# SBUF placement of the streamed and the stationary operands in a two-stack transformer kernel

## What is computed

```python
# first_block, 2 layers
a = rms_norm(h, attn_norm[i]); proj = a @ w_in[i]
mix = concat([diff_attention(...), ssd_mixer(...), gla_mixer(...)])
h = h + mix @ w_out[i]
f = rms_norm(h, ffn_norm[i])
h = h + (silu(f @ w_ffn_gate[i]) * (f @ w_ffn_up[i])) @ w_ffn_down[i]
h = h + sigmoid(h @ ple_w_gate[i]) * (p[i] @ ple_w_proj[i])
# second_block, 4 layers (stick-breaking, MoBA, sliding window, stick-breaking)
mod = silu(c) @ ada_w[i] + ada_b[i]            # shift, scale, gate, twice
x = x + g1 * attention(modulate(rms_norm(x), sh1, sc1))
x = x + g2 * swiglu(modulate(rms_norm(x), sh2, sc2), w_gate, w_up, w_down)
```

## Time and profile before

| | |
|---|---|
| median of 3 runs | 2531.91 us (2529.34 to 2535.33) |
| the profiled execution's own time | 2530.38 us |
| its span, first to last instruction | 2528.6 us |
| mean granted TensorE clock | 0.933 of full |
| PE busy | 92% of the span |
| PEld busy | 85% |
| DVE busy | 59% |
| ACT busy | 40% |
| DMA | 56% of 16 engines, 173 GB/s |

### The profile page before, as it was taken

The page is one execution under the profiler, slowest core; times in us unless marked ns, Lnnn a source line. Parts: engine busy times, 40 slices in busy tenths (PEclk is TensorE's granted clock), DMA queues, the critical chain, the costliest instruction groups (busy, mean ns, idle before and its releaser), DMA issues.

```text
span 2528.6 us, 44727 instructions
## 1 busy us (share of the span) xinstructions
PE 2320.7 (92%) x17136; PEld 2153.3 (85%) x17136; DVE 1500.3 (59%) x2564; ACT 1020.5 (40%) x1670; POOL 0.2 (0%) x4
## 2 busy tenths in 40 slices
PE   5799899988798899899899989899978899998998
PEld 4687699987786799879899978799966799897998
DVE  4533178845431488836688876587866555566554
ACT  3412244414321344325544444444444444455443
POOL 0000000000000000000000000000000000000000
PEclk8989799998988899999899989899988899998999
DMA  4344179962433299844389954389932366443664
GB/s 130 96 108 108 34 243 297 305 198 84 125 85 101 68 306 301 276 122 129 94 268 303 300 161 125 98 289 296 289 113 68 118 191 192 124 133 100 191 193 139
DMA packets 553295, 436.26 MB, mean 173 GB/s; under 512 B 31824, under 2 KB 479352, under 8 KB 553080
## 3 DMA queue, kind: packets, MB, share of 16 engines
q1 hardware_dynamic: 549840, 431.35, 56.0%
q10 hardware_dynamic: 3368, 3.71, 0.5%
HBM read 433.96 MB, written 1.05 MB: 172 GB/s over the span
## 4 chain that ended last, share of the span: by engine, by line
PE 84%; DVE 7%; ACT 3%; DMA 2%; issue 2%; DVEq 1%; ACTq 1%; SPq 0%
PE bank L575 12%; PE bank L576 12%; PE bank L577 12%; PE acc L575 6%; PE acc L576 6%; PE acc L577 6%; PE bank L561 6%; PE bank L702 5%; PE acc L620 3%; PE bank L980 2%; PE bank L779 2%; PE bank L585 1%; PE bank L570 1%; PE bank L745 1%; PE bank L691 1%
## 5 line engine op out<-in xcount | busy, mean ns | idle before, releaser
L575 PE MATMUL bank<-h_hi,w_hi 128*128 128x256 f32 x2704 | 775.0, 287 | 27.4 <-DVE h_lo L1251 15.2
L576 PE MATMUL bank<-h_lo,w_hi 128*128 128x256 f32 x2704 | 761.6, 282 | 0.0
L577 PE MATMUL bank<-h_hi,w_lo 128*128 128x256 f32 x2704 | 760.4, 281 | 0.0
L1013 ACT ACTIVATE w_hi<-wslot 128x1024 fp32r<-128x1024 f32 x510 | 531.3, 1056 | 509.8 <-PE acc L577 261.5
L1429 DVE TENSOR_TENSOR w_lo<-wslot,w_hi 128x1024 fp32r<-128x1024 f32 x396 | 474.7, 1221 | 229.5 <-ACT w_hi L1013 229.1
L575 PEld LDWEIGHTS bank<-h_hi,w_hi 128*128 128x128 f32 x2704 | 520.6, 193 | 46.6 <-issue 31.9
L576 PEld LDWEIGHTS bank<-h_lo,w_hi 128*128 128x128 f32 x2704 | 522.4, 193 | 0.0
L577 PEld LDWEIGHTS bank<-h_hi,w_lo 128*128 128x128 f32 x2704 | 521.9, 193 | 0.0
L575 PE MATMUL acc<-mid_hi,w_hi 128*128 128x256 f32 x1056 | 299.0, 283 | 0.8 <-DVE mid_lo L1662 0.8
L576 PE MATMUL acc<-mid_lo,w_hi 128*128 128x256 f32 x1056 | 295.5, 280 | 0.0
L577 PE MATMUL acc<-mid_hi,w_lo 128*128 128x256 f32 x1056 | 295.2, 280 | 0.0
(11 more groups left out here) (255 smaller groups left out, 2688.4 us busy)
## 6 DMA issues: line engine op xcount, KB each, us to landing
wslot<-in_ada_w_dram SPq DMA_DIRECT2D x192, 512.0 KB, 5.9
wslot<-in_ffn_w_gate_dram SPq DMA_DIRECT2D x88, 512.0 KB, 4.7
wslot<-in_ffn_w_up_dram SPq DMA_DIRECT2D x88, 512.0 KB, 5.4
wslot<-in_ffn_w_down_dram SPq DMA_DIRECT2D x88, 512.0 KB, 3.6
wslot<-in_w_in_dram SPq DMA_DIRECT2D x72, 512.0 KB, 4.1
wslot<-in_sb_w_in_dram SPq DMA_DIRECT2D x48, 512.0 KB, 4.6
wslot<-in_w_ffn_gate_dram SPq DMA_DIRECT2D x44, 512.0 KB, 4.9
wslot<-in_w_ffn_up_dram SPq DMA_DIRECT2D x44, 512.0 KB, 5.5
```

The source lines that it names most:

```text
L575: pe.matmul(dst, w_hi[:, w, cols], hi, start=start, stop=False, skip_group_check=True)
L576: pe.matmul(dst, w_hi[:, w, cols], lo, start=False, stop=False, skip_group_check=True)
L577: return pe.matmul(dst, w_lo[:, w, cols], hi, start=False, stop=stop, skip_group_check=True)
L1013: return act.activation(dst, src, ACT.Copy)
```

## The change

The order of the `sb(...)` calls is changed; no instruction, shape, wait or transfer is added or removed. Sizes rounded up to 32 bytes, small tiles move between the streamed families.

```diff
-        cum = sb("cum", [P, 8])
         mid_hi = sb("mid_hi", [P, 2, S], F32R)
         mid_lo = sb("mid_lo", [P, 2, S], F32R)
-        wend = sb("wend", [P, 4])
+        dt_bias = sb("dt_bias", [P, DEPTH, 8])
+        a_neg = sb("a_neg", [P, DEPTH, 8])
+        h_lo = sb("h_lo", [P, KT, S], F32R)
+        sinks = sb("sinks", [P, 16])
+        a_log = sb("a_log", [P, DEPTH, 8])
         h_hi = sb("h_hi", [P, KT, S], F32R)
-        h_lo = sb("h_lo", [P, KT, S], F32R)
-        wexp = sb("wexp", [P, 4])
+        skip_all = sb("skip_all", [P, DEPTH, 8])
+        lam = sb("lam", [P, DEPTH, 4])
+        neg_lam = sb("neg_lam", [P, DEPTH])
         y_hi = sb("y_hi", [P, 512], F32R)
         y_lo = sb("y_lo", [P, 512], F32R)
-        epst = sb("epst", [P, 1])
+        da_gain = sb("da_gain", [P, DEPTH])
+        skip = sb("skip", [P, DEPTH, 4])
         w_hi = sb("w_hi", [P, PART_DOWN + 1, D], F32R)
         w_lo = sb("w_lo", [P, PART_DOWN + 1, D], F32R)
         const = sb("const", [P, table_dram.shape[1]])
```

More of the change, by code:

```diff
@@ L270, in two_stacks @@
         lam_tmp = sb("lam_tmp", [P, DEPTH, 2, 64])
[L271 to L275, removed]
         wg2 = sb("wg2", [16, DEPTH, 256])
[L277 to L280, removed]
         c_act = sb("c_act", [P, KT])
@@ L299, in two_stacks @@
         dts = sb("dts", [P, 8, 8])
+        cum = sb("cum", [P, 8])
         dif, mt = (sqT[:, 4 * n:4 * n + 4, :].rearrange("p (t a) s -> p t (a s)", t=TT) for n in range(2))
+        wend = sb("wend", [P, 4])
+        wexp = sb("wexp", [P, 4])
         st_sb = pt[:, 0, :]
         zero = sb("zero", [1, 512], BF16)
+        epst = sb("epst", [P, 1])
         acc = ctx.enter_context(nc.psum_tensor("acc", [P, KT, S], F32))
```

## The result

The changed kernel takes 2551.46 us in the median of 4 runs (2548.44 to 2554.18), against 2530.62 us for the kernel before in the same comparison: a ratio of 1.009, with a 95% interval of 1.0072 to 1.0108 (the two medians alone give 1.008). It is slower by 0.8 to 0.9%, outside the range. The time lies near that of the second rival, which had been priced at 2548 us; the terms behind that price came out otherwise, as the part on the prediction shows.

The account below looks back on a forecast made before the run. PE, busy without a break in the FFNs, was taken as the bound, through its matmuls' pitch. Terms of −13.3 (mid) and −3.0 (y) summed to −16.3 us, taking 2531.9 to 2515.6 us; range 2498 to 2534 us.

Parts of the forecast that it names:

- rival 2: Distance modulo 512 counts and h slows to 117.5 ns: +32.7 − 16.3 = +16.4 us, 2548 us; 15%.
- What bounds it: In the FFNs PE runs without a break at full clock; the change can only work through the matmuls' pitch.
- h, "I take 0": h matmuls stay at 64 modulo 128, so 0; bounds a gain of 10.9 us and a loss of 32.7 us.
- mid, −13.3 us: 3168 mid matmuls take h's pitch of 113.3 ns, 4.2 ns less each; bounds 0 and 17.7 us.
- y, −3.0 us: 760 full-clock y matmuls gain 5.3 ns each, 4.0 us, three quarters counted; bounds 0 and 5.1 us.
- const, writers, parameters, DMA: Plain float32 table matmuls, DVE writes, small-parameter loads and FFN DMA cover: each taken as no change in time.
- The sum: −13.3 for mid and −3.0 for y give −16.3 us: from 2531.9 to 2515.6 us.
- Rival 1: Nothing moves, 2531.9 us: mid's and y's excess comes from writing eight places of acc in turn; 14%.
- Rival 3: Every family reaches the weight-load floor of about 111.9 ns: 33.7 us less, 2498 us; 12%.
- Rival 4: In the four loaded FFNs DMA turns 8.9 us of mid's gain into wslot waits: 2524.5 us; 6%.

Follow-up runs that it names:

- e5: Kernel before with h_hi and h_lo both at 320 from the weights modulo 512, y at 0, mid still at 416; 2557.64 us.
- e6: Kernel before with h_hi and h_lo both at 192 from the weights modulo 512, y at 64, mid at 416; 2532.28 us.
- e8: Kernel before with h_hi and h_lo at 0 from the weights modulo 512, y at 32, mid at 416; 2576.04 us.
- e1: Kernel before with mid and y moved by 32 bytes each, so mid, h and y all lie at 448 modulo 512; 2536.66 us, ratio 1.0026.
- e3: Kernel before with h alone moved, h_hi to 320 and h_lo to 192 from the weights; 2561.92 us.
- e15: Kernel before with mid and y at 32 from the weights, h at 448; 2525.33 us, ratio 0.9981.
- e7: Kernel before with h_hi left at 448, h_lo alone at 192, y at 384, mid at 416; 2528.57 us.
- e4: Kernel before with mid, h, y, weights and const all moved by 128 bytes, distances kept; 2532.59 us.
- e2: Changed kernel with h put back to 448 from the weights, mid at 64; 2542.74 us.
- e9: Kernel before with y at 448 and, in the two unloaded FFNs, mid written to the y tiles at 448; 2524.12 us, ratio 0.9974.
- e10: All families at 448 as in e1, with the L585 sums put after down instead of ahead of it; 2539.28 us, ratio 1.0047.

## Why the prediction was wrong, point by point

- **What bounds it.** Right: PE's pitch at full clock, with no new wait and DMA below its share before.
- **h, "I take 0".** This is the step that failed. The reason given, a pitch set by the distance modulo 128, is refuted by e5 against e6: 320 and 192 are both 64 modulo 128 and give 117.8 and 113.8. The distances tried fit a period of 256. The upper bound in the same line, h at 117.5, is the pace that h took. Its 32.7 us were too much for the changed kernel: start to start, its h matmuls take 25.1 us more than before (21.5 in the FFNs, 3.6 outside). The price put every h matmul at 113.3, but behind a mid run the first tile of h took 2.75 us already before, 114.6 ns a matmul. The argument against rival 2, that 416 and 480 next to 448 are bad and so the period looks like 64 or 128, was no argument: three distances within 64 bytes tell of the width of the good place, not of its period. The fourth point of that order, plain float32 at distance 0, was no like case: it streams 128 columns, and float32r at 0 is the slowest place of all (e8, 120.0 ns).
- **mid, −13.3 us.** Also failed, by the same step: 64 modulo 512 is 64 modulo 256, a bad place (117.9). In place of a gain of 13.3 us it is 3168 x 0.4 ns = 1.3 us of loss by the pitch, 0.8 us start to start. And the good place would not have given it either: at 448 (e1) mid fell to 117.8 in the loaded FFNs and took h along. A pitch was carried from one family to another as if it belonged to the distance alone.
- **y, −3.0 us.** The sign was right, by luck: the reason was 64 modulo 128, and y at 64 modulo 512, which meets that too, stays at 117.5 (e6). The change happened to put y at 448, the distance of h before. The size was too large: at 448 a little over half of the y runs at full clock go at 113.3 to 114 (13 of 23 or 24, by where full clock is cut off) and the others near 117.8. 760 x 13 / 23 x 5 ns is some 2 us; start to start y takes 1.4 us less.
- **const, writers, parameters, DMA.** Right at 0: L585 has 46.1 us in place of 46.0, the load behind its eight still starts 0.89 us after the first, L678 20.6 for 20.5, DVE on `y_lo` 422 ns for 422, the wait at L634 6.1 for 6.2.
- **The sum.** Rival 2 had +32.7 − 16.3 = +16.4, near the +20.8 of the medians, but its terms were not those: h cost 25.1, and mid and y together gave 0.6 instead of 16.3. The nearness of 2548 to 2551.5 is in part luck, and the period is not 512, since 192 is as good as 448. In the two profiled executions the spans differ by 18.1 us: +22.4 in the FFNs, +3.6 for h outside them, −1.4 for y, and −6.4 for all other instructions (968.0 to 961.6 us). Those others are the same in number. The execution before spent 342 us of its span at half the clock and the one after 307 (mean granted clock 0.933 and 0.940), which is enough to cover the 6.4 us (an estimate: half of the 35 us, some 17 us, is the most that it can be worth); that it is the reason is likely and not shown.
- **Rival 1, and the rule behind it.** Refuted: e3, e5 and e8 change nothing but places and cost 30 to 48 us. The Trainium skill (SBUF — State Buffer, "Who interferes with whom") has PE's two read ports independent and PE never waiting on anyone, by which the place of the tiles would not count; here, with a load of weights at each matmul next to a stream of 256 columns, the place alone moves the pitch from 113.3 to 120.0 ns, and the measurement decides. What happens at the ports no trace shows. The part of rival 1 about `acc` is refuted too: mid into `acc` reaches 113.3 in e1.
- **Rival 3, the floor.** No float32r run was clearly below 113.3; the 1.4 ns above the weight loads stayed. **Rival 4** did not arise.

## What to carry to other kernels

Where each matmul loads its weights and PE is at 100%, look at the count of instructions in a fixed stretch, not at the busy share: it shows a few ns in the pitch that the busy share hides. A layout in SBUF is then a parameter to be measured, for all families together and with several distances apart by 64 to 256 bytes, since one seen distance does not give the period, and the pace of a family can hang on what runs ahead of it. A family at a place that is never the best (here mid at 416 or 32) can be worth more than one at the best place, because it resets the one behind it: e1, with all three families at 448, is slower than the kernel before.

## What the runs showed of the hardware that was not expected

- Float32r matmuls of 128x128 weights with 256 streamed columns, each with its own load, run at full clock between 113.3 and 120.0 ns by the distance of the streamed tile from the weights. Modulo 256, 192 gives 113.3 or 117.8 (e1), 0 gives 120 (e8), 32 from 116.5 (e15), 64 from 117.5 to 118 (e5, e6), 128 gives 118.8 (e7), 160 gives 117.4 in the kernel before and up to 118.9 in e3, and 224 gives 118.3 (before). The absolute place, moved by 128 bytes, does not count (e4).
- At 192 there are two stable paces, 113.3 and 117.8 ns, that last through whole FFNs (e1, e2, e9, e10). What passes the pace on, and why L585 leaves 117.8 in 39 of 40 cases (e1), the profile does not show; a conflict between the two reads would be one explanation, and is only argued.
- At a distance of 0 plain float32 runs that stream 128 columns go at 111.7 to 111.9 ns (L702, where the chain of the changed kernel has 1.79 us for 16, as in the earlier trace rows), where float32r with 256 columns takes 120 (e8). Type and columns differ together, so which of them matters is open.
